# Projections in tiles of 512 columns and half the features, with four sums open

## The reference

```python
n = rms_norm(h, norm_mix_g)
z, xbc, dt_raw, q, k, v = split(n @ w_in)          # 512, 1024, 8, 512, 512, 512 columns
y_ssd = ssd_mixer(z, xbc, dt_raw, ...)             # 8 heads, chunked scan
q = rope(rms_norm(q, q_norm_g), cos, sin)          # per head of 64; k in the same way
y_diff = diff_attention(q, k, v, ...)              # 4 heads, softmax(s1) - lam * softmax(s2)
h = h + concat([y_ssd, y_diff]) @ w_out
h = h + peer_ffn(rms_norm(h, norm_ffn_g), ...)     # 8 heads, top 16 of 128 x 128 experts
e = rms_norm(p @ ple_proj, ple_norm_g)
gate = sigmoid(rms_norm(h, ple_gate_norm_g) @ ple_gate_w)
h = h + gate * e
```

## Time and profile before

| | us |
|---|---|
| median of 3 runs | 1677.86 (1676.59 to 1679.01) |
| the profiled execution, its own time | 1684.69 |
| its span, from the first to the last instruction | 1682.7 |
| PE busy | 1605.2 (95%) |
| PEld busy | 1454.4 (86%) |
| VectorE busy | 1157.3 (69%) |
| GpSimd busy | 1075.9 (64%) |
| ScalarE busy | 622.0 (37%) |
| mean granted clock of TensorE | 0.983 |

### The profile page before, as it was taken

How to read it: one execution, slowest core, us unless ns; L and a number is a source line. 1 busy time by engine, 2 the same in 40 slices (tenths; PEclk the granted TensorE clock), 3 DMA queues, 4 the chain that set the end, 5 groups by cost and what they waited for, 6 DMA issues and landing times.

```text
span 1682.7 us, 26153 instructions
## 1 busy us (share of the span) xinstructions
PE 1605.2 (95%) x9085; PEld 1454.4 (86%) x9085; DVE 1157.3 (69%) x2501; ACT 622.0 (37%) x909; POOL 1075.9 (64%) x550
## 2 busy tenths in 40 slices
PE   7999878999799989899999999999999999999998
PEld 6799747977799989899999999978888888888888
DVE  6772574400879999968999998256676676767756
ACT  3133464200233323245556555433333333333331
POOL 5453302553358767767666666668988888888953
PEclk9999979999899999999999999999999999999999
DMA  5221113320358878768999998899999999999961
GB/s 198 76 80 72 46 43 117 137 89 25 104 190 288 286 241 280 245 219 282 354 336 340 340 347 321 311 359 368 366 349 364 350 360 361 351 358 357 343 233 44
DMA packets 172513, 417.74 MB, mean 248 GB/s; under 512 B 13088, under 2 KB 97696, under 8 KB 167328
## 3 DMA queue, kind: packets, MB, share of 16 engines
q1 hardware_dynamic: 133856, 257.52, 43.7%
q0 software_dynamic: 36864, 134.23, 22.8%
q10 hardware_dynamic: 1728, 25.17, 3.9%
HBM read 360.25 MB, written 56.62 MB: 248 GB/s over the span
## 4 chain that ended last, share of the span: by engine, by line
PE 38%; issue 18%; DVE 9%; POOL 7%; DMA 2%; SPq 0%; ACT 0%; POOLq 0%; DVEq 0%
PE s_psum L1340 29%; PE s_psum L1294 5%; POOL h L1252 3%; POOL s_lo L1243 2%; DMA scores<-gate_scratch 1%; DVE h L1477 1%; POOL s_more_rows L1252 1%; PE s_psum L196 1%; DVE s_besti L1515 1%; DVE s_gtile L1509 1%; DVE s_besti L1506 1%; PE s_psum L197 1%; PE s_psum L198 1%; DVE s_gtile L1503 1%; DVE s_gtile L1512 1%
## 5 line engine op out<-in xcount | busy, mean ns | idle before, releaser
L1243 POOL TENSOR_TENSOR s_lo<-s_raw,s_hi 128x1024 fp32r<-128x1024 f32 x224 | 548.3, 2449 | 225.8 <-ACT s_hi L1376 222.5
L1294 PE MATMUL s_psum<-hn_hi,s_hi 128*128 128x384 f32 x1024 | 351.0, 343 | 26.8 <-POOL s_lo L1243 26.8
L1376 ACT CAST s_hi<-s_raw 128x1024 fp32r<-128x1024 f32 x256 | 267.7, 1048 | 288.1 <-PE s_psum L1340 217.4
L1294 PE MATMUL s_psum<-hn_lo,s_hi 128*128 128x384 f32 x1024 | 345.5, 337 | 0.0
L1294 PE MATMUL s_psum<-hn_hi,s_lo 128*128 128x384 f32 x1024 | 345.4, 337 | 0.0
L1340 PE MATMUL s_psum<-s_hi,s_whi 128*128 128x512 f32 x768 | 300.5, 391 | 4.3 <-DVE s_wlo L1635 2.2
L1340 PE MATMUL s_psum<-s_hi,s_wlo 128*128 128x512 f32 x768 | 299.9, 391 | 0.0
L1340 PE MATMUL s_psum<-s_lo,s_whi 128*128 128x512 f32 x768 | 299.9, 391 | 0.0
L1294 PEld LDWEIGHTS s_psum<-hn_hi,s_hi 128*128 128x128 f32 x1024 | 195.0, 190 | 30.2 <-POOL s_lo L1243 29.9
L1277 POOL DMA_INDIRECT s_gtile<-in_v_t,s_v_row x128 | 201.4, 1573 | 25.0 <-issue 23.6
L1294 PEld LDWEIGHTS s_psum<-hn_lo,s_hi 128*128 128x128 f32 x1024 | 195.1, 191 | 0.0
(11 more groups left out here) (295 smaller groups left out, 2779.9 us busy)
## 6 DMA issues: line engine op xcount, KB each, us to landing
s_raw<-in_u_t SPq DMA_DIRECT2D x128, 512.0 KB, 5.0
s_raw<-in_v_t SPq DMA_DIRECT2D x128, 512.0 KB, 7.1
act_scratch<-s_acts SPq DMA_DIRECT2D x128, 192.0 KB, 3.8
gate_scratch<-s_gtile ACTq DMA_DIRECT2D x12, 2048.0 KB, 10.5
scores<-act_scratch SPq DMA_DIRECT2D x32, 768.0 KB, 7.0
...
```

Source lines behind the costliest of these rows:

```text
L1243: pool.tensor_tensor(lo[:, s, :], raw[:, s, :], hi[:, s, :].bitcast(F32), ALU.subtract).then_inc(lo_ready[s], 1)
L1294: last = pe.matmul(psU[:, s % 2, :], uu[:, s, d * P:(d + 1) * P], hh[:, d, P:T], start=(n == 0 and d == 0), stop=(n == 2 and d == DC - 1))
L1376: act.copy(hi[:, s, :], raw[:, s, :]).then_inc(hi_ready[s], 1)
```

## The change

The weights of q, k, v, z, the output projection and the gates are laid out anew: a tile of 1 MB now holds half of the features (4 chunks) and 512 columns instead of all features and 256 columns. Two tiles make one set of four sums of 512 columns. `product_by_halves` opens the four sums (one bank for each token tile) with the first half of the features and closes them with the second; a sum is done only in the second half. `half_product` makes 12 matmuls of 512 columns. The number of weight tiles, their size, loads, cuts and drains stay. xBC, dt and the retrieval's queries stay as they were.

All readers get 512 columns: the squares and roots of q and k, the copies of v and z, the sums into h and the squares behind them. The rotary sum has no free half of the bank any more: the sine parts are made first into `ropeB`, then the cosine product overwrites the bank in place, then the sum. In the gates ScalarE, VectorE and SP still work in pieces of 256 columns, two for each bank. The transposes of dt get their own place ahead of q in the list of banks.

```diff
     return last
+WIDE, DEPTH = 512, DC // 2
+def wide(part):
+    return part.rearrange("p c n -> p (c n)").rearrange("p (c n) -> p c n", c=DEPTH)
+def half_product(pe, out, left, right, half, made=None):
+    for d in range(DEPTH):
+        at, first, final = half * DEPTH + d, half == d == 0, half == 1 and d == DEPTH - 1
+        if made:
+            pe.wait_ge(made[0], made[1] + at + 1)
+        pe.matmul(out, left(0, at), right(0, d), start=first, stop=False)
+        pe.matmul(out, left(0, at), right(1, d), start=False, stop=False)
+        last = pe.matmul(out, left(1, at), right(0, d), start=False, stop=final)
+    return last
+def product_by_halves(pe, weights, n, banks, left, done, made=None):
+    for half in range(2):
+        w = [wide(part) for part in weights.ready(pe, n + half)]
+        for t in range(TB):
+            out = banks.take(pe, *done[t]) if half == 0 else banks.at(*done[t])
+            last = half_product(pe, out, lambda part, d: left(part, d, t), lambda part, d: w[part][:, d, :], half,
+                                made if t == 0 else None)
+            if half:
+                last.then_inc(banks.done, 1)
+            yield half, t
+        pe.drain().then_inc(weights.used[(n + half) % 2], 1)
...
+    out += [(("dt", 0), "dtraw_done", 1)]
     for name, ready in (("q", "qk_ready"), ("k", "qk_ready"), ("v", "v_ready")):
-        base = 2 * TB if name == "k" else 0
-        out += [((name, i), ready, base + i + 1) for i in range(2 * TB)]
-        if name == "q":
-            out.insert(-2 * TB + 1, (("dt", 0), "dtraw_done", 1))
+        base = TB if name == "k" else 0
+        out += [((name, t), ready, base + t + 1) for t in range(TB)]
     for t in range(TB):
         out += [(("xsT", t), "xs_ready", t + 1), (("bT", t), "btok_ready", t + 1)]
...
     out += [(("yT", c), "nT_ready", DC + c + 1) for c in range(DC)]
-    out += [(("h", i), "h_ready", i + 1) for i in range(4 * TB)]
+    out += [(("h", i), "h_ready", i + 1) for i in range(2 * TB)]
...
-            def project(n, name, half, t):
-                w = weights.ready(pe, n)
-                out = bank.take(pe, name, half * TB + t)[:, 0:256]
-                tile_done(product(pe, out, lambda part, d: nT[part][:, d, t * P:(t + 1) * P], lambda part, d: w[part][:, d, :]))
-            for n in range(XBC_C // 2, N_IN - 2):
-                for t in range(TB):
-                    project(n, "qkv"[(n - 4) // 2], n % 2, t)
-                    if n == XBC_C // 2 and t == 0:
+            nT_of = lambda part, d, t: nT[part][:, d, t * P:(t + 1) * P]
+            for i, name in enumerate("qkv"):
...
+                out = bank.take(pe, "z", t)
                 for half in range(2):
-                    project(N_IN - 2 + half, "z", half, t)
+                    w = [wide(part) for part in weights.ready(pe, N_IN - 2 + half)]
+                    last = half_product(pe, out, lambda part, d: nT_of(part, d, t), lambda part, d: w[part][:, d, :], half)
                     if t == TB - 1:
                         pe.drain().then_inc(weights.used[(N_IN - 2 + half) % 2], 1)
+                tile_done(last)
                 pe.wait_ge(sem["xdt_ready"], 2 * t + 1)
                 pe.wait_ge(sem["m_ready"], 2 * t + 2)
...
-            for n in range(4):
-                w = weights.ready(pe, N_OUT + n)
-                for t in range(TB):
-                    out = bank.take(pe, "h", n * TB + t)[:, 0:256]
-                    tile_done(product(pe, out, lambda part, d: nT[part][:, d, t * P:(t + 1) * P], lambda part, d: w[part][:, d, :],
-                                      made=(sem["nT_ready"], DC) if n == t == 0 else None))
-                pe.drain().then_inc(weights.used[(N_OUT + n) % 2], 1)
+            for n in range(2):
+                for _ in product_by_halves(pe, weights, N_OUT + 2 * n, bank, nT_of, [("h", n * TB + t) for t in range(TB)],
+                                           made=(sem["nT_ready"], DC) if n == 0 else None):
+                    pass
...
-                src = bank.filled(act, "qk"[i // (2 * TB)], i % (2 * TB))[:, 0:256]
+                src = bank.filled(act, "qk"[i // TB], i % TB)
                 if i:
                     act.wait_ge(sem["qksum_ready"], i)
-                me.did(act.activation(sqj[:, 0:256], src, ACT.Square), sem["qksq_ready"])
+                me.did(act.activation(sqj[:, :], src, ACT.Square), sem["qksq_ready"])
                 act.wait_ge(sem["qksum_ready"], i + 1)
...
-            for i in range(4 * TB):
+            for i in range(2 * TB):
                 n, t = i // TB, i % TB
                 act.wait_ge(sem["h_ready"], i + 1)
-                me.did(act.activation(xn(t)[:, n * 256:(n + 1) * 256], h[:, t, n * 256:(n + 1) * 256], ACT.Square, accum_out=hsq[:, t, n:n + 1]), sem["hsq_ready"])
-                if n == 3:
+                cs = slice(n * WIDE, (n + 1) * WIDE)
+                me.did(act.activation(xn(t)[:, cs], h[:, t, cs], ACT.Square, accum_out=hsq[:, t, n:n + 1]), sem["hsq_ready"])
+                if n == 1:
                     act.wait_ge(sem["hsum_ready"], t + 1)
                     me.did(act.activation(hst[:, 2, t:t + 1], hst[:, 0, t:t + 1], ACT.Sqrt, scale=1.0 / D, bias=eps), sem["hroot_ready"])
...
-            for i in range(4 * TB):
-                w, half, t = i // (2 * TB), i // TB % 2, i % TB
-                src = bank.filled(dve, "qk"[w], half * TB + t)[:, 0:256]
+            for i in range(2 * TB):
+                w, t = i // TB, i % TB
+                src = bank.filled(dve, "qk"[w], t)
                 dve.wait_ge(sem["qksq_ready"], i + 1)
-                me.did(dve.tensor_reduce(qks[:, 2, i, :], sqj[:, 0:256].rearrange("p (h d) -> p h d", d=HD), AX.X, ALU.add), sem["qksum_ready"])
+                me.did(dve.tensor_reduce(qks[:, 2, i, :], sqj.rearrange("p (h d) -> p h d", d=HD), AX.X, ALU.add), sem["qksum_ready"])
                 two = lambda ap: ap.rearrange("p (h two r) -> p h two r", two=2, r=32)
-                ra, rb = bank.at("qk"[w], half * TB + t)[:, 256:512], ropeB[:, i % 2, 0:256]
-                q4, a4, b4 = two(src), two(ra), two(rb)
-                cosg = tab[:, 2 * w, t, :, :].unsqueeze(1).to_broadcast([P, 4, 2, 32])
-                me.did(dve.tensor_tensor(a4, q4, cosg, ALU.mult))
+                other = ropeB[:, i % 2, :]
                 for side in range(2):
-                    sing = tab[:, 2 * w + 1, t, side, :].unsqueeze(1).to_broadcast([P, 4, 32])
-                    me.did(dve.tensor_tensor(b4[:, :, side, :], q4[:, :, 1 - side, :], sing, ALU.mult))
+                    sing = tab[:, 2 * w + 1, t, side, :].unsqueeze(1).to_broadcast([P, 8, 32])
+                    me.did(dve.tensor_tensor(two(other)[:, :, side, :], two(src)[:, :, 1 - side, :], sing, ALU.mult))
                 me.settle()
-                step(dve.tensor_tensor(ra, ra, rb, ALU.add))
+                cosg = tab[:, 2 * w, t, :, :].unsqueeze(1).to_broadcast([P, 8, 2, 32])
+                step(dve.tensor_tensor(two(src), two(src), cosg, ALU.mult))
+                step(dve.tensor_tensor(src, src, other, ALU.add))
                 dve.wait_ge(sem["qkroot_ready"], i + 1)
                 step(dve.reciprocal(qks[:, 3, i, :], qks[:, 1, i, :]))
-                step(dve.tensor_tensor(qn[:, t, w, half * 256:(half + 1) * 256].rearrange("p (h d) -> p h d", d=HD),
-                                       ra.rearrange("p (h d) -> p h d", d=HD), spread_last(qks[:, 3, i, :], HD), ALU.mult), sem["qk_ready"])
+                heads = lambda ap: ap.rearrange("p (h d) -> p h d", d=HD)
...
-            for n in range(4):
+            for n in range(2):
                 for t in range(TB):
-                    src = bank.filled(dve, "h", n * TB + t)[:, 0:256]
-                    hv = h[:, t, n * 256:(n + 1) * 256]
+                    src = bank.filled(dve, "h", n * TB + t)
+                    hv = h[:, t, n * WIDE:(n + 1) * WIDE]
                     me.did(dve.tensor_tensor(hv, hv, src, ALU.add), sem["h_ready"])
-                    if n == 3:
+                    if n == 1:
...
-            for n in range(4):
-                w = g_weights.ready(pe, n)
-                for t in range(TB):
-                    out_ = bank.take(pe, "g", n * TB + t)[:, 0:256]
-                    last = product(pe, out_, lambda part, d: nT[part][:, d, t * P:(t + 1) * P], lambda part, d: w[part][:, d, :],
-                                   made=(sem["nT_ready"], 0) if n == t == 0 else None)
-                    last.then_inc(sem["pe_tile"], 1)
-                pe.drain().then_inc(g_weights.used[n % 2], 1)
+            nT_of = lambda part, d, t: nT[part][:, d, t * P:(t + 1) * P]
+            for n in range(2):
+                for _ in product_by_halves(pe, g_weights, 2 * n, bank, nT_of, [("g", n * TB + t) for t in range(TB)],
+                                           made=(sem["nT_ready"], 0) if n == 0 else None):
+                    pass
...
```

(6 more changed lines are left out.)

54 lines of the change are left out of this document (28 added, 26 removed).

## The result

The changed kernel took 1684.13 us (median of 9 runs, 1682.56 to 1688.53) beside 1677.86 for the kernel before (9 runs): a ratio of 1.0039 (1.0028 to 1.0051), 6.3 us slower. The forecast was 1675.7 with a range up to 1680.0. The same two kernels, timed again in another set of runs, gave 1682.13 beside 1680.39, a ratio of 1.0006 (0.9993 to 1.0019). The mean of the two ratios, weighted by their errors, is 1.0024, 4.0 us slower. Since the two intervals don't overlap, the error of that mean is better judged by their distance, some 3 us either way. The later sets of runs were taken on chips 10, 11 and 1 (the chip of the first set is not on record), and the kernel before alone had medians of 1677.9, 1678.9, 1681.1 and 1680.4 us in the four sets.

What follows compares the result with a forecast made beforehand. TensorE's stream was taken to set the pace where the change acts. The terms, 2.3 + 2.6 - 4.3 - 1.7 + 3.3, gave 2.2 us gained: 1677.86 - 2.2 = 1675.7 us, range 1671.4 to 1680.0.

Steps and rivals of the forecast that it cites:

- Term 1: q, k, v, z stream: 0.29 us saved on each of eight weight tiles, 2.3 us gained (1.1 to 3.6).
- Term 2: Output projection: shorter tiles and no start waits in the first token tile, 2.6 us gained (2.2 to 3.1).
- Term 3: Behind output projection: GpSimd's cuts delay last normalising to s + 18.9 (s: fourth tile's start), 4.3 us lost.
- Term 4: Behind the normalising: TensorE's pause of some 3.4 us lowers its granted clock, 1.7 us lost (0 to 5).
- Term 5: Gate projection: stream 4.7 us shorter, tail 1.3 longer, net 3.3 us gained (2.0 to 3.3).
- (b): Rival, behind output projection: normalising not held up, tail costs 1.5 and no clock; 6.7 us gained, 1671.2; chance 0.15.
- (d): Rival, wide projections: a 512-column matmul costs two of 256; 3.7 us lost, 1681.6; chance 0.12.
- (a): Rival, behind output projection: the pause is there but the clock holds; 3.9 us gained, 1674.0; chance 0.17.
- (c): Rival, behind the pause: clock stays low much longer, costing 5 instead of 1.7; 1.1 us lost, 1679.0; chance 0.10.
- The sign that the prediction set for a reason not seen: Scores stage or value loop changing by more than 1 us would make the forecast wrong for an unseen reason.

Runs made afterwards that it cites:

- late_cut: The changed kernel, with GpSimd's second query weight cut waiting until all four token tiles are normalised: 1677.7 us beside 1681.1 for the kernel before, ratio 0.9982.
- act_norm: The changed kernel, with the normalising moved from VectorE to ScalarE: 1675.17 us beside 1681.1 for the kernel before, ratio 0.9963; timed again 1677.61, ratio 0.9983.
- after_again: The changed kernel without further edit, timed once more: 1682.13 us beside 1680.39 for the kernel before, ratio 1.0006.
- no_out: The changed kernel with the output projection back at 256 columns: 1678.33 us, ratio 0.9989 to the kernel before.
- only_gate: The kernel before with only the gates' projection made wide: 1679.13 us, ratio 0.9998.
- only_out: The kernel before with only the output projection made wide: 1686.24 us beside 1678.9, ratio 1.0038.
- act_norm_before: The kernel before, with the normalising moved from VectorE to ScalarE: 1678.83 us, ratio 0.9990.
- only_qkvz: The kernel before with only q, k, v and z made wide: 1681.03 us, ratio 1.0014; timed again, ratio 1.0000.

## Why the prediction was wrong, point by point

The forecast was 2.2 us faster; the stages say 4.0 slower and the first ratio 6.3 slower. What it said of the mechanism came true almost to the row: the late normalising, its length, the clock behind it, the two gains. Two steps failed. The first is terms put at nothing, the start of the experts' block (+1.4) and the attention stage (+1.3), together 2.7 us. The second is sizes: the clock's price (1.7 instead of 2.8), the saving of the stream (2.3 instead of 1.5) and the last stage (3.3 instead of 2.2). The 2 us by which the first set of runs lies above the stages belong to no term: the second set lies 3 us below them.

**Term 1 (-2.3), mis-sized.** The stage gained 1.5 us, inside the bounds of 1.1 to 3.6. A tile of q, k or v takes (139.96 - 93.32) / 4 = 11.66 us against 11.84 over five tiles in the earlier trace rows (11.79 to 11.90, mean 11.83, in the six profiles with narrow ones), 0.17 a tile, near the low end of the bounds. The step that failed is taking the pitch of the 512-column product from another stage (11.39) and averaging: the pitch, the time from one matmul's start to the next, goes with the stage as much as with the width (512 columns: 11.66 us a tile here, 11.39 in the queries). The rule that was set aside did better here. The Trainium skill (TensorE: Matmul & The Clock Gate, "Wait — 56ns, not 53.3ns?") gives about 2.5 ns for each matmul beside its columns; 48 fewer in a tile are 0.12 us by that rule, an estimate. The traces come near it in q, k, v (0.17) and in the output projection (11.85 to 11.70, 0.15). In the gates a tile went from 12.01 to 11.41, 0.6 us, and there it does not hold.

**Term 2 (-2.6), nearly right.** From the first matmul to the fourth tile, as the forecast counts, it is 309.13 - 274.11 = 35.02 us against 37.26, 2.2 us gained; with the fourth tile, as the table counts, 2.3. Both lie in its bounds. The start waits are gone as forecast (first tile 285.83 - 274.11 = 11.72, like the others), the pitch gave 0.15 instead of 0.3 a tile.

**Term 3 (+4.3), right.** With s = 309.13 the last normalising ends at 328.22 = s + 19.1, where the prediction has 18.9, and lasts 2.84 us where 2 to 3 were forecast. The first query product comes at s + 21.2 instead of s + 16.7 before, 4.5 us later; measured from the transposes' start, as the table counts, it is +4.6 (9.43 against 4.82). late_cut and act_norm show that the cut is the cause. The Trainium skill (GPSIMD Engine Reference, section 1, Specifications) says which of VectorE's instructions contend with GpSimd; by that rule the adds with an input in PSUM stay free, and they do: 0.69 us at 312.23, inside the low cut, and 0.67 at 323.20, inside the next.

**Term 4 (+1.7), right in kind, mis-sized.** The first query tile lost 2.8 us. The forecast took 8 us at 0.79 from the earlier trace rows, 1.7 us of low clock; the three windows above have 0.66, 0.50 and 0.99, that is 3.4 us, twice as much, with dense matmuls in all but the first. A stretch of another stage was a poor measure for it.

**Term 5 (-3.3), right for its stream, mis-sized for the stage.** Timelines of TensorE, VectorE and ScalarE in the changed kernel, beside the earlier trace rows:

```profile
1630.81 0.47 PE L216 MATMUL s_psum<-e_w_hi,e_nT_hi 128*128 128x512 f32 x1 [0.89 <-DVE e_nT_lo L1736]
1642.20 0.47 PE L216 MATMUL s_psum<-e_w_hi,e_nT_hi 128*128 128x512 f32 x1 [0.24 <-issue]
1653.63 0.47 PE L216 MATMUL s_psum<-e_w_hi,e_nT_hi 128*128 128x512 f32 x1 [0.26 <-issue]
```

```profile
1655.93 4.71 DVE L1749 TENSOR_TENSOR h<-h,e_gate 128x256 f32<-128x256 f32 x1
...
1678.40 0.42 DVE L1749 TENSOR_TENSOR h<-h,e_gate 128x256 f32<-128x256 f32 x1
```

```profile
1676.06 0.84 ACT L1498 ACTIVATE e_gate<-s_psum,e_st 128x256 f32<-128x256 f32 x2 [1.88 <-PE s_psum L218]
```

Tiles of 11.39 and 11.43; VectorE ends 2.76 us behind the start of the last sigmoids against 1.46 before, the 1.3 us of the forecast; the sum at 1655.93 is held 4.71 us by the low cut from 1655.70 to 1660.34, and the delay is worked off. From the first gate product to VectorE's last sum it is 48.0 us against 51.3, 3.3 as forecast. But the first product itself came later after the value loop in this kernel (5.6 us behind its last matmul, 6.0 in after_again, 4.8 before), so the whole stage gained 2.2; in late_cut, act_norm and no_out it gained 3.3. VectorE's rows show what it waited for:

```profile
1621.49 1.29 DVE L1689 SCALAR_TENSOR_TENSOR s_psum<-s_gtile,s_w,s_psum 128x1024 f32<-128x1024 f32 x1 [1.31 <-DMA s_gtile<-in_v_t,s_v_row]
...
1624.12 3.67 DVE L1733 TENSOR_TENSOR h<-h,s_psum 128x512 f32<-128x512 f32 x6
```

The last gathered rows of values landed late, so the last work on them started 3.7 us ahead of the value loop's last matmul (8.4 in the first profile of before), the sums into h (L1733) 1.05 us ahead of it instead of 2.90, and the transposes for the gates wait for these sums. The same holds for after_again and only_gate (3.3 and 2.3 us ahead) and for none of the eleven others (6.0 to 9.1). Since only_gate has it too and late_cut doesn't, it looks like chance in the landing of the gathers; that was not tested.

**What the sum left out.** Two terms, both on work that the diff does not touch. The way to the first expert score grew by 1.4 us. The DMA view from 438 to 450 us, of after_again (queue: packets, MB, share; then the issues with the median us to landing) and below it of only_out, where SP issues the same four loads at the same time (441.8):

```profile
q1 hardware_dynamic: 576, 2.10, 49.3%
q8 instruction: 1, 0.02, 0.5%
q14 instruction: 1, 0.01, 0.2%
...
s_raw<-in_u_t SPq DMA_DIRECT2D x5, 512.0 KB, 5.4
```

```profile
q1 hardware_dynamic: 586, 2.14, 50.0%
...
s_raw<-in_u_t SPq DMA_DIRECT2D x5, 512.0 KB, 4.3
```

The expert rows land 1.1 us later in the one that also loads code there (the queues of kind "instruction"), and ScalarE's first cast follows at 446.28 against 445.21. All five profiles with both the wide q, k, v, z and the wide output projection have this column 1.1 to 1.7 us longer, and act_norm_before has 0.9. In just these six a packet of code starts within 3 us behind SP's first issue of the expert rows, and the first cast starts 4.0 to 5.0 us behind that issue; in the eight others no such packet lies there, and the cast comes at 3.2 to 3.5 us. That the loading of code causes it fits all fourteen, but no run was made to test it. And the attention stage took 1.3 us more than before's mean, with its mean clock at 0.81 in both profiles of the changed kernel and at 0.81, 0.90 and 0.86 in the three of before. Over all kernels with wide q, k, v, z the stage spreads from 76.7 to 78.3 (mean 77.4), over the others from 75.9 to 78.2 (mean 76.9), so half of this term or more may be chance.

**The rivals.** (b), L1020 not held up, is refuted by its 2.84 us, and (d), a wide matmul as dear as two narrow ones, by tiles of 11.66 us. (a) is refuted: the clock fell. (c) named the side but priced the clock at 5 where it was 2.8. The forecast's mechanisms all appeared; the sum missed by 0.8 (term 1), 0.3 (term 2), 0.3 (term 3), 1.1 (term 4), 1.1 (term 5), and by 1.4 + 1.3 for what it left out: together 6.3, which but for rounding leads from -2.2 to +4.0. The sign that the prediction set for a reason not seen, over 1 us in the scores stage, did show: from the first expert score to the value loop it is 646.7 and 646.9 us against 650.2, 648.8 and 650.2. But that is a gain, and among the kernels whose code there is the same it spreads from 645.0 to 650.2, so it says nothing about the change.

The range was too narrow for a second reason: it held nothing for the spread of stages that the change doesn't touch, which in these profiles is larger than most terms.

**Open.** Why the start of the experts' block is later (the loading of code fits), why wide q, k, v and z go with more low clock, and why ratios move between sets of runs. Also open is the value loop of only_qkvz: 532.3 and 531.2 us in its two profiles and 527.6 to 529.8 in all others. In both, TensorE waits twice for over 1 us, for VectorE's low part, within the first 36 us of the loop, here in the first:

```profile
1103.58 0.50 PE L1368 MATMUL s_psum<-s_hi,s_whi 128*128 128x512 f32 x1 [2.06 <-DVE s_lo L1695]
...
1123.21 0.79 PE L1368 MATMUL s_psum<-s_hi,s_whi 128*128 128x512 f32 x1 [2.73 <-DVE s_lo L1695]
```

The twelve others have one such wait there, of 1.5 to 3.7 us. Why the loop starts with two in this kernel, and not in no_out, is not shown.
